# Three edits to an eight-core decoder step: the bias matmul's rows, a run of matmuls in an early wait, and who scales the last output

## The chip, the cores and the metric

The kernel runs on all 8 cores of one Trainium2 chip. All cores run the same program on their own data, without talking to each other: core i has prompt i of 2,048 tokens and 16 of the 128 running sequences with 8 new tokens each, 2,176 tokens in all. The metric is the device time in microseconds of the slowest core. Before the change it is 1296.83 us, the median of 3 runs from 1296.55 to 1297.41.

## The reference

One step of a two-layer trunk of width 1024. Every sub-layer works on a normalised and modulated input, and its result goes back through a gate:

```python
def modulate(x, g, shift, scale):
    return rms_norm(x, g) * (1 + scale) + shift
# per layer i; sh, sc, g come from silu(c) @ w_ada[i] + b_ada[i]
h = modulate(x, norm_g[i, 0], sh1, sc1)
y = pool_mixer(...)  if i == 0 else  sgu_mixer(...)
x = x + g1 * y
h = modulate(x, norm_g[i, 1], sh2, sc2)
x = x + g2 * (relu(h @ w1) ** 2) @ w2          # w1 1024x4096, w2 4096x1024
# at the end
return rms_norm(x, final_g)
```

Layer 0 mixes tokens by trailing-window means. Layer 1 mixes them by the spatial gating mixer, whose first step matters here:

```python
z = jax.nn.gelu(h @ w_in + b_in)               # w_in 1024x2048, b_in 2048
u, v = jnp.split(z, 2, axis=-1)
v = layer_norm(v, ln_g, ln_b)
mixed = w_eff @ v + b_sp                       # per chunk of 128 tokens, causal
y = (u * mixed) @ w_out
```

## The kernel before, in words

The activations x stay in SBUF for the whole kernel, as 8 blocks of 128 channels by 2,176 tokens in float32. h lies beside it in bf16. The tokens are cut into five groups (`GR`): 0 of 384, 1 and 2 of 512, 3 of 384, and 4 of 384, of which the last 128 are the running sequences. Weights come in pieces of 128x4096 through a ring of six buffers, loaded by GpSimd's DMA queue (POOL) in the fixed order of `PIECES`. A piece can be asked for when the piece that had its buffer is used up.

No engine's order is written by hand. Every operation is a node with a cost, a due time (`S.base`, or the running clock `S.clk` of matmul work) and optionally an earliest time. `schedule()` simulates all engines with these costs and picks, on each engine, the node with the lowest due time among those that could start first. The result is a fixed order for each engine, with semaphore waits for the data dependences. The planner's times are not on the chip; only the order is.

The start: groups 0 and 1 of x and the modulation pieces are loaded. `ada_piece` is 32 matmuls of 17 columns over one piece, followed by vector operations that write `modT`. Pieces (0,2) and (0,3) are the first two, then comes the small piece `wpool`, and then (0,4) is the third. ScalarE multiplies the pooling weights by the modulation (line 885), into a ring buffer (`wAvb`), and `pool_mm` (line 858) uses them. `h2_prompt` then forms the input of the channel MLP, whose first piece of w1 is used by line 1019.

The middle: the channel MLP of each layer runs in 8 blocks of 512 hidden units, over the five groups (`mlp`). `mm1` (line 1019) is 4 chains of 8 matmuls; ScalarE applies ReLU (line 1025) and the square (line 1027). `mm2` (line 1045) is 8 chains of 4 matmuls, and VectorE adds each into x (line 755). `weave` interleaves the `mm1` of one group with the `mm2` of the group before.

`v_tile` computes the v half of the gating mixer for 128 tokens at a time, in two halves of 512 channels: 8 matmuls of 128 rows (line 1201), then one matmul that adds the bias row to every token (line 1203). Its stationary operand is one row of ones and its moving operand one row of 512 bias values. There are 17 tiles, so 34 such matmuls. `binv` is loaded by one DMA of one row (line 1143).

`stats` squares x on ScalarE and sums over channels by a matmul with ones. In the `summed` form GpSimd adds the 8 squares in float32 (line 644), and a single matmul follows (line 646). In the other form 8 matmuls take the 8 squares (line 652). ScalarE's Ln and Exp give the reciprocal root: in PSUM for the summed form (lines 658 and 661), in SBUF for the other (`rstd` or `R1s`, lines 671 and 674).

The end: the last block goes over the groups in the order 4, 1, 2, 0, 3. After `mm2` of a group comes `final` for it: `stats`, then on VectorE `x * final_g * R` for each of the 8 channel blocks (line 1327), and a DMA for each pair of blocks (line 1331). Group 3 is split there into 256 and 128 tokens.

Of the kernel before, what the change touches and what calls it, by code (L numbers as in the profile page):

```python
# [380 lines left out]
def c_act(n):  # L381
    return 0.07 + n * 0.00085
# [10 lines left out]
def c_stt(n):  # L393
    return 0.13 + n * 0.00103
# [14 lines left out]
def build_program():  # L409
# [29 lines left out]
    def sb(name, shape, dt):  # L439
        return nc.alloc_sbuf_tensor(name, list(shape), dt)  # L440
# [25 lines left out]
    def AR(lo, hi):  # L466
        return ("ar", lo, hi)
# [17 lines left out]
    def P_(v):  # L485
        return ps[v.slot].ap()
# [35 lines left out]
    S.op("sp", lambda e: e.dma_start(out=vecs.ap(), in_=d_vecs.ap()), writes=VR, stream="s_vecs", cost=0.1, nbytes=196608)  # L522
    S.op("dve", lambda e: e.memset(ones.ap(), 1.0), writes=[("ones", 0, 1)])
    S.op("dve", lambda e: e.memset(mhalf.ap(), -0.5), writes=[("mhalf", 0, 1)], cost=0.1)
    S.op("dve", lambda e: e.memset(epsd.ap(), float(D * EPS)), writes=[("epsd", 0, 1)], cost=0.1)
# [101 lines left out]

    def stats(t0, n, own=False, summed=False):

# [25 lines left out]
        ch = S.chain(mms, v)  # L655
        if summed:
            RK = [(v.key, 0, 1)]
            ev = S.op("act", lambda e: e.activation(out=P_(v)[:, 0:n], in_=P_(v)[:, 0:n], func=AF.Ln, bias=epsd.ap()[:, 0:1], scale=1.0),
                      reads=[(v.key, 0, 1), ("epsd", 0, 1)], writes=RK, cost=c_act(n), vbs=[v], table="ln")
            S.evac(ch, ev)  # L660
            ev.glue = S.op("act", lambda e: e.activation(out=P_(v)[:, 0:n], in_=P_(v)[:, 0:n], func=AF.Exp, scale=-0.5),
                           reads=RK, writes=RK, cost=c_act(n), vbs=[v], table="ln")
            return Bank(v, 0, n), RK
        ri = rsi[0]
# [84 lines left out]
    def resid(l, vG, v, dco, t0, n, s0, s1):  # L749
# [8 lines left out]
        if s1 > s0:  # L758
# [311 lines left out]
    def mlp(l, after=None, hooks=None, first=None):  # L1070
# [5 lines left out]
        for (b, g) in steps:  # L1076
# [17 lines left out]
            else:  # L1094
                m1 = mm1(l, b, (hb(g), n, 0), ao, n)
                m2 = mm2(l, b, t0, n if g < 4 else 256, 256 if g == 4 else 0, 384 if g == 4 else 0, ao, n, 0)
                weave(m1, pend)
                if b == 7 and prevg is not None and after is not None:
# [35 lines left out]
    def sgu_setup():  # L1134
# [48 lines left out]
    def v_tile(g, tt):  # L1183
# [12 lines left out]
        for hf in range(2):  # L1196
# [5 lines left out]
                    [(pvb.key, 0, 1)] + HK(c0, c0 + 128, [dc]), 512) for dc in range(NDC)]  # L1202
            mms.append((lambda e, hf=hf, v=v: e.matmul(P_(v), ones.ap()[0:1, :], binv[0:1, hf * 512:(hf + 1) * 512], start=False, stop=True),  # L1203
                        [AR(BINV, BINV + 2048), ("ones", 0, 1)], 512))
            ch = S.chain(mms, v, vbs=[pvb])
# [89 lines left out]
    def sgu():  # L1295
# [19 lines left out]
        norm(1, 1, 4)  # L1315

    def final(g, off=0, nn=None, own=False):
        t0, n = GR[g]
        t0 += off
        if nn is not None:  # L1320
            n = nn
        R, RK = stats(t0, n, own, summed=nn is None and g != 0)
        for d in range(0, NDC, 2):
            S.base = S.clk + 30.0
            for dc in (d, d + 1):
                xs = xT.ap()[:, dc, t0:t0 + n]
                S.op("dve", lambda e, xs=xs, dc=dc: e.scalar_tensor_tensor(out=xs, in0=xs, scalar=vcol(VFG + dc), in1=R.ap(), op0=ALU.mult, op1=ALU.mult),  # L1327
                     reads=XK(t0, t0 + n, [dc]) + RK + VR, writes=XK(t0, t0 + n, [dc]), cost=c_stt(n), vbs=R.vbs)
            oo = 8 * t0 + d * n
            S.base = None  # L1330
            S.op("sp", lambda e, d=d, oo=oo: e.dma_start(out=o_y.ap()[:, oo:oo + 2 * n].rearrange("p (c t) -> p c t", t=n), in_=xT.ap()[:, d:d + 2, t0:t0 + n]),
                 reads=XK(t0, t0 + n, [d, d + 1]), stream="o_y", cost=0.1, nbytes=1024 * n)
# [89 lines left out]
```

How the kernel before makes its waits and increments, by code:

```python
                def body(eng, ops=seq[e], e=e):  # L356
                    for n in ops:
                        ins = None
                        for (emit, w) in n.swaits:
                            for d in w:
                                eng.wait_ge(d.sigval[0], d.sigval[1])
                            ins = emit(eng)
                        if n.stream is not None:
                            ins.then_inc(n.sigval[0], 16)
                        elif n.sig:
                            ins.then_inc(n.sigval[0], 1)
                    if e == "sp":
                        for (sem, val) in final:
                            eng.wait_ge(sem, val)
                        for e2 in ENGS:
                            if e2 != e and cnt[e2] > 0:
                                eng.wait_ge(esem[e2], cnt[e2])
```

## Time and profile before

| | before |
|---|---|
| median of 3 runs | 1296.83 us |
| the profiled execution's own time | 1297.52 us |
| its span, slowest core (5) | 1295.9 us |
| spans of the 8 cores | 1293.8 to 1295.9 us |
| busy: TensorE | 95% |
| busy: VectorE | 60% |
| busy: ScalarE | 45% |
| busy: GpSimd | 11% |

The span is the time from the first to the last instruction of a core; 1.6 us of the execution lie around it. The profile cuts the span into 40 slices of 32.4 us:

```profile
PE   2689999999999999999999999999999999999995
DVE  3488775544455454569777768754545455454577
ACT  3367543333333333377444666433333333333474
PEclk9799999999999999999999999999999999999997
DMA  9999586535253433311100035420303031200025
```

Each digit is a busy share in tenths; PEclk is the granted clock of TensorE. The first three slices and the last have an idle TensorE, and the DMA engines are busy throughout the first four. All rows below are of core 5, the slowest, unless they say otherwise.

### The profile page before, as it was taken

What the parts mean: (1) busy time and instruction counts of PE and PEld (TensorE: products, weight loads), DVE (VectorE), ACT (ScalarE), POOL (GpSimd) and SP (SyncE); (2) the same over time, 40 slices, a digit from 0 to 9 for tenths busy, and PEclk for the clock granted to TensorE, in tenths of its full rate; (3) what the DMA queues carried; (4) which work ended last, traced back from release to release, by engine and by line L of the source; (5) the groups of instructions that cost most, each with busy time, mean ns of one, the idle gap of its engine ahead of it and who ended that gap; (6) DMA issues with size and microseconds to landing.
All of it is one profiled execution on the core that took longest, in us unless ns stands there. A gap on an engine that the chain in (4) does not pass through costs nothing.

```text
span 1295.9 us, 21767 instructions; the slowest of 8 cores (1293.8 to 1295.9 us)
## 1 busy us (share of the span) xinstructions
PE 1236.4 (95%) x7481; PEld 662.2 (51%) x7481; DVE 771.3 (60%) x1482; ACT 584.1 (45%) x1084; POOL 138.5 (11%) x169
## 2 busy tenths in 40 slices
PE   2689999999999999999999999999999999999995
PEld 0345565555555555545444455554555555454543
DVE  3488775544455454569777768754545455454577
ACT  3367543333333333377444666433333333333474
POOL 2100000000000000055221230000000000000060
PEclk9799999999999999999999999999999999999997
DMA  9999586535253433311100035420303031200025
GB/s 199 215 215 171 90 121 102 95 61 89 51 95 58 73 66 66 66 33 34 33 1 1 1 65 97 100 47 19 66 1 66 1 65 31 35 2 1 1 88 190
DMA packets 20842, 91.08 MB, mean 70 GB/s; under 512 B 2768, under 2 KB 7168, under 8 KB 12656
## 3 DMA queue, kind: packets, MB, share of 16 engines
q0 software_dynamic: 11552, 76.26, 33.3%
q1 hardware_dynamic: 9184, 13.43, 3.5%
q8 instruction: 64, 1.05, 0.3%
q14 instruction: 42, 0.34, 0.1%
HBM read 145.43 MB, written 11.01 MB: 121 GB/s over the span
## 4 chain that ended last, share of the span: by engine, by line
PE 89%; DVE 3%; DMA 3%; issue 2%; ACT 1%; POOL 1%; DVEq 0%; ACTq 0%; POOLq 0%
PE ps L1019 36%; PE ps L1045 35%; PE ps L1288 5%; PE ps L1201 4%; PE ps L1171 3%; DMA ring<-w_pack 3%; PE ps L858 2%; PE ps L652 1%; PE ps L595 1%; PE ps L1203 1%; DVE hT_sb L721 1%; DVE xT_sb L1327 1%; DVE hT_sb L708 1%; PE ps L1254 1%; DVE xT_sb L755 1%
## 5 line engine op out<-in xcount | busy, mean ns | idle before, releaser
L755 DVE SCALAR_TENSOR_TENSOR xT_sb<-ps,modT,xT_sb 128x384 f32<-128x384 f32 (+3 forms) x728 | 458.2, 637 | 426.0 <-PE ps L1045 379.5
L1019 PE MATMUL ps<-hT_sb,ring 128*128 128x384 bf16 (+2 forms) x2592 | 522.1, 346 | 2.8 <-ACT hT_sb L718 2.5
L1045 PE MATMUL ps<-arena,ring 128*128 128x384 bf16 (+3 forms) x2624 | 522.3, 343 | 1.7 <-DVE xT_sb L755 1.6
L1025 ACT ACTIVATE arena<-ps 128x384 bf16<-128x384 f32 (+3 forms) x324 | 170.0, 527 | 490.8 <-PE ps L1019 490.8
L1045 PEld LDWEIGHTS ps<-arena,ring 128*128 128x128 bf16 x2624 | 253.7, 98 | 218.2 <-issue 3.2
L1019 PEld LDWEIGHTS ps<-hT_sb,ring 128*128 128x128 bf16 x2592 | 251.4, 98 | 220.6 <-issue 5.1
L1027 ACT ACTIVATE arena<-arena 128x384 bf16<-128x384 bf16 (+3 forms) x324 | 181.2, 562 | 27.2
L570 POOL DMA_DIRECT2D ring<-w_pack x62 | 33.3, 538 | 850.0 <-PE ps L595 336.3
L644 POOL TENSOR_TENSOR sq<-sq 128x512 f32<-128x512 f32 (+3 forms) x77 | 88.7, 1152 | 181.6 <-ACT sq L640 175.7
L640 ACT ACTIVATE sq<-xT_sb 128x512 f32<-128x512 f32 (+1 forms) x88 | 50.3, 579 | 47.0 <-DVE xT_sb L755 31.8
L649 ACT ACTIVATE sq<-xT_sb 128x384 bf16<-128x384 f32 (+3 forms) x128 | 57.9, 500 | 22.2 <-DVE xT_sb L755 15.2
L1201 PE MATMUL ps<-ring,hT_sb 128*128 128x512 bf16 x272 | 64.4, 380 | 0.0
L1171 PE MATMUL ps<-hT_sb,ring 128*128 128x384 bf16 (+1 forms) x320 | 62.6, 347 | 0.0
L1288 PE MATMUL ps<-arena,ring 128*128 128x384 bf16 (+1 forms) x320 | 60.0, 347 | 0.0
L708 DVE TENSOR_TENSOR hT_sb<-xT_sb,rstd 128x768 bf16<-128x768 f32 (+2 forms) x48 | 44.3, 973 | 17.6 <-ACT rstd L674 17.6
L652 PE MATMUL ps<-sq,ones 128*128 128x384 bf16 (+3 forms) x128 | 27.9, 339 | 22.1 <-ACT sq L649 20.6
L1288 PEld LDWEIGHTS ps<-arena,ring 128*128 128x128 bf16 x320 | 31.1, 98 | 27.8 <-issue 0.7
L768 DVE TENSOR_TENSOR xT_sb<-xT_sb,arena 128x128 f32<-128x128 f32 x136 | 40.2, 298 | 7.0 <-DVE arena L765 0.9
L1171 PEld LDWEIGHTS ps<-hT_sb,ring 128*128 128x128 bf16 x320 | 30.6, 98 | 25.3 <-issue 0.5
L718 ACT ACTIVATE hT_sb<-hT_sb,modT 128x384 bf16<-128x384 bf16 (+2 forms) x60 | 39.6, 723 | 5.2 <-DVE modT L603 2.7
L1201 PEld LDWEIGHTS ps<-ring,hT_sb 128*128 128x128 bf16 x272 | 24.6, 98 | 29.3 <-issue 4.3
L765 DVE TENSOR_TENSOR arena<-ps,modT 128x128 f32<-128x128 f32 x136 | 38.0, 281 | 2.7 <-PE ps L1045 2.6
(103 smaller groups left out, 533.0 us busy)
## 6 DMA issues: line engine op xcount, KB each, us to landing
ring<-w_pack POOLq DMA_DIRECT2D x62, 1024.0 KB, 10.3
xT_sb<-x_pack POOLq DMA_DIRECT2D x3, 1536.0 KB, 39.1
xT_sb<-x_pack POOLq DMA_DIRECT2D x2, 2048.0 KB, 35.1
y_pack<-xT_sb SPq DMA_DIRECT2D x8, 512.0 KB, 2.8
y_pack<-xT_sb SPq DMA_DIRECT2D x8, 384.0 KB, 3.0
ring<-w_pool POOLq DMA_DIRECT2D x1, 1024.0 KB, 33.3
y_pack<-xT_sb SPq DMA_DIRECT2D x4, 256.0 KB, 2.9
arena<-sp_pack POOLq DMA_DIRECT2D x1, 736.0 KB, 17.1
```

The lines of the kernel that those rows point to most:

```text
L640: S.op("act", lambda e, si=si, dc=dc: e.activation(out=fs[si], in_=xT.ap()[:, dc, t0:t0 + n], func=AF.Square), reads=XK(t0, t0 + n, [dc]), ...
L644: S.op("pool", lambda e, si=si, o=o: e.tensor_tensor(out=o, in0=fs[a], in1=fs[si], op=ALU.add), reads=fk[a] + fk[si], writes=k, cost=c_poo ...
L649: S.op("act", lambda e, si=si, dc=dc: e.activation(out=sqt.ap()[:, si * 512:si * 512 + n], in_=xT.ap()[:, dc, t0:t0 + n], func=AF.Square), ...
L708: S.op("dve", lambda e, d=d: e.tensor_tensor(out=hT.ap()[:, d:d + step, c0:c0 + n], in0=xT.ap()[:, d:d + step, t0:t0 + n], in1=rb(R, step) ...
L755: nodes.append(S.op("dve", lambda e: e.scalar_tensor_tensor(out=xs, in0=P_(v)[:, 0:n], scalar=mcol(l, vG, dco), in1=xs, op0=ALU.mult, op1= ...
L1019: mms = [(lambda e, dc=dc: e.matmul(P_(v)[:, 0:n], pv(key, 512)[:, dc, fc * 128:(fc + 1) * 128], hT.ap()[:, dc, c0:c0 + n], start=(dc == 0 ...
L1025: ev = S.op("act", lambda e: e.activation(out=av, in_=P_(v)[:, 0:n], func=AF.Relu), reads=[(v.key, 0, 1)], writes=ak, cost=c_act(n), vbs=[v])
L1027: S.op("act", lambda e: e.activation(out=av, in_=av, func=AF.Square), reads=ak, writes=ak, cost=c_act(n) + 0.03)
L1045: mms.append((lambda e, fc=fc, av=av: e.matmul(P_(v)[:, 0:w], pv(key, 1024)[:, fc, dco * 128:(dco + 1) * 128], av, start=(fc == 0), stop=( ...
L1171: mms = [(lambda e, dc=dc, key=key, fc=fc, v=v: e.matmul(P_(v)[:, 0:n], pv(key, 512)[:, dc, (fc % 4) * 128:(fc % 4 + 1) * 128], hT.ap()[:, ...
L1201: mms = [(lambda e, dc=dc, key=key, v=v: e.matmul(P_(v), hT.ap()[:, dc, c0:c0 + 128], pv(key, 512)[:, dc, :], start=(dc == 0), stop=False) ...
L1288: mms.append((lambda e, cc=cc, uv=uv, key=key, dco=dco, v=v: e.matmul(P_(v)[:, 0:n], pv(key, 512)[:, cc, (dco % 4) * 128:(dco % 4 + 1) * 1 ...
```

## The change

- **Bias.** A new tile `first` of 128x128 has ones in row 0 and zeros elsewhere. It is the stationary operand of the bias matmul, in place of one row of ones. The moving operand is `binv` with 128 rows, which one DMA fills by reading the bias row 128 times.
- **Matmuls in a wait.** `keep_busy(32)` adds one chain of 32 matmuls of ones by ones, 512 columns each, into a PSUM bank that nobody reads. Its due and earliest time in the plan is 31.0, ahead of the third modulation piece (32.0).
- **Last output.** All `final` calls now keep R in PSUM. For group 2 the sum of squares no longer goes through GpSimd. For blocks 6 and 7 of group 2 and 4 to 7 of group 0, ScalarE multiplies by `final_g` and GpSimd by a second copy of R in SBUF; VectorE keeps the rest. In the last step of the last block `mm2` of group 0 runs ahead of `mm1` of group 3 and is no longer woven with it.

```diff
+    S.op("dve", lambda e: e.memset(first.ap(), 0.0), writes=[("first", 0, 1)], cost=0.2)
+    S.op("dve", lambda e: e.memset(first.ap()[0:1, :], 1.0), reads=[("first", 0, 1)], writes=[("first", 0, 1)], cost=0.1)
...
-    def stats(t0, n, own=False, summed=False):
+    def stats(t0, n, own=False, summed=False, bank=None, both=False):
...
-        if summed:
+        if summed if bank is None else bank:
             RK = [(v.key, 0, 1)]
             ev = S.op("act", lambda e: e.activation(out=P_(v)[:, 0:n], in_=P_(v)[:, 0:n], func=AF.Ln, bias=epsd.ap()[:, 0:1], scale=1.0),
...
+            if both:
+                ri = rsi[0]
+                rsi[0] = 1 - ri
+                ro, rk = rstd[ri].ap()[:, 0:n], [(("rstd", ri), 0, 512)]
+                ev.glue = S.op("act", lambda e: e.activation(out=ro, in_=P_(v)[:, 0:n], func=AF.Exp, scale=-0.5),
+                               reads=RK, writes=rk, cost=c_act(n), vbs=[v], table="ln")
+                ev = ev.glue
...
+    def keep_busy(k):
+
+        v = S.vb("ps")
+        S.chain([(lambda e, v=v: e.matmul(P_(v), ones.ap(), bcast(ones.ap(), [0, 4], [1, 128]), start=True, stop=True),
+                  [("ones", 0, 1)], 512) for _ in range(k)], v)
...
+    S.base, S.earliest = 31.0, 31.0
+    keep_busy(32)
+    S.earliest = 0.0
     for a, b in ((4, 32.0), (5, 36.0), (8, 57.0), (9, 63.0), (6, 70.0), (7, 77.0)):
...
-                weave(m1, pend)
+                if l == 1 and b == 7 and g == 3:
+                    for f in pend + m1:
+                        f()
+                else:
+                    weave(m1, pend)
...
-        S.op("pool", lambda e: e.dma_start(out=binv[0:1, :], in_=d_binv.ap()), writes=[AR(BINV, BINV + 2048)], stream="s_binv", cost=0.53, nbytes=4096)
+        S.op("pool", lambda e: e.dma_start(out=binv, in_=bass.AP(d_binv, 0, [[0, 128], [1, 1024]])), writes=[AR(BINV, BINV + 2048)], stream="s_binv", cost=0.53, nbytes=4096)
...
-            mms.append((lambda e, hf=hf, v=v: e.matmul(P_(v), ones.ap()[0:1, :], binv[0:1, hf * 512:(hf + 1) * 512], start=False, stop=True),
-                        [AR(BINV, BINV + 2048), ("ones", 0, 1)], 512))
+            mms.append((lambda e, hf=hf, v=v: e.matmul(P_(v), first.ap(), binv[:, hf * 512:(hf + 1) * 512], start=False, stop=True),
+                        [AR(BINV, BINV + 2048), ("first", 0, 1)], 512))
...
+    SHARE = {2: (6, 7), 0: (4, 5, 6, 7)}
...
-        R, RK = stats(t0, n, own, summed=nn is None and g != 0)
+        share = SHARE.get(g, ()) if nn is None else ()
+        if share:
+            (R, RK), (Rp, RPK) = stats(t0, n, summed=False, bank=True, both=True)
+        else:
+            R, RK = stats(t0, n, own, summed=nn is None and g in (4, 1), bank=True)
...
+                if dc in share:
+                    S.base = S.clk + 20.0
+                    S.op("act", lambda e, xs=xs, dc=dc: e.activation(out=xs, in_=xs, func=AF.Identity, scale=vcol(VFG + dc)),
+                         reads=xk + VR, writes=xk, cost=c_act(n) + 0.05)
+                    S.op("pool", lambda e, xs=xs: e.tensor_tensor(out=xs, in0=xs, in1=Rp.ap(), op=ALU.mult), reads=xk + RPK, writes=xk, cost=c_pool(n))
+                    S.base = S.clk + 30.0
+                    continue
```

## Rows read from the trace of the kernel before

**Rows 1.** The page: busy time by engine, and the chain that ended last by engine.

```profile
PE 1236.4 (95%) x7481; PEld 662.2 (51%) x7481; DVE 771.3 (60%) x1482; ACT 584.1 (45%) x1084; POOL 138.5 (11%) x169
...
PE 89%; DVE 3%; DMA 3%; issue 2%; ACT 1%; POOL 1%; DVEq 0%; ACTq 0%; POOLq 0%
```

**Rows 2.** TensorE's timeline: start us, us, instruction, count, and idle before with its releaser.

```profile
609.84 1.89 PE L1201 MATMUL ps<-ring,hT_sb 128*128 128x512 bf16 x8
611.66 0.39 PE L1203 MATMUL ps<-arena,ones 1*128 1x512 bf16 x1
611.98 1.90 PE L1201 MATMUL ps<-ring,hT_sb 128*128 128x512 bf16 x8
```

**Rows 3.** Line 1203: count, duration ns min/median/max, first and last start.

```profile
L1203 PE MATMUL ps<-arena,ones x34: 384/385/385, 611.7 to 778.0; 1*128 1x512 bf16 x34
```

**Rows 4.** TensorE's timeline: a lone matmul of 128 rows, and what follows it.

```profile
1266.71 0.38 PE L646 MATMUL ps<-sq,ones 128*128 128x512 bf16 x1
1266.93 1.46 PE L1045 MATMUL ps<-arena,ring 128*128 128x384 bf16 x8
```

**Rows 5.** TensorE's waits from 190 to 1260 us; and its timeline at 625.

```profile
PE ps L652 <- DVE arena L1272: 1.4, 1, 1.4
...
625.31 0.32 PE L646 MATMUL ps<-sq,ones 128*128 128x384 bf16 x1 [0.76 <-POOL sq L644]
```

**Rows 6.** TensorE's timeline around the third modulation piece.

```profile
34.85 1.00 PE L595 MATMUL ps<-siluT,ring 128*128 128x17 bf16 x32 [5.12 <-DMA ring<-w_pack]
45.05 1.00 PE L595 MATMUL ps<-siluT,ring 128*128 128x17 bf16 x32 [9.20 <-DMA ring<-w_pack]
46.91 0.48 PE L858 MATMUL ps<-hT_sb,ring 128*128 128x384 bf16 x1 [0.86 <-ACT ring L885]
```

**Rows 7.** Windows: length, TensorE busy (count), granted clock, DMA share, GB/s.

```profile
45.00:50.00 5.00, 3.77 (x44) 0.50 0.98 234
50.00:51.00 1.00, 1.00 (x9) 0.90 0.89 315
91.00:94.50 3.50, 3.50 (x14) 0.52 1.03 343
```

**Rows 8.** ScalarE's timeline: the pooling weights.

```profile
46.26 6.50 ACT L885 ACTIVATE ring<-ring,Aw 128x256 bf16<-128x256 f32 x16 [17.93 <-PE ps L595]
```

**Rows 9.** First w1 piece: GpSimd's issue, its landing (us), TensorE's first use.

```profile
55.18 0.53 POOL L570 DMA_DIRECT2D ring<-w_pack  x1 [1.36 <-PE ps L595]
...
ring<-w_pack POOLq DMA_DIRECT2D x1, 1024.0 KB, 34.9
...
90.24 4.42 PE L1019 MATMUL ps<-hT_sb,ring 128*128 128x384 bf16 x16 [2.50 <-ACT hT_sb L718]
```

**Rows 10.** The same first use on core 6, in TensorE's timeline.

```profile
88.94 2.76 PE L1019 MATMUL ps<-hT_sb,ring 128*128 128x384 bf16 x16 [2.35 <-DMA ring<-w_pack]
```

**Rows 11.** VectorE's timeline at the end.

```profile
1267.85 1.27 DVE L755 SCALAR_TENSOR_TENSOR xT_sb<-ps,modT,xT_sb 128x384 f32<-128x384 f32 x2 [1.55 <-PE ps L1045]
1269.03 2.06 DVE L1327 SCALAR_TENSOR_TENSOR xT_sb<-xT_sb,vecs_sb,ps 128x512 f32<-128x512 f32 x3
...
1275.99 3.33 DVE L755 SCALAR_TENSOR_TENSOR xT_sb<-ps,modT,xT_sb 128x256 f32<-128x256 f32 x11
...
1280.55 7.48 DVE L1327 SCALAR_TENSOR_TENSOR xT_sb<-xT_sb,vecs_sb,rstd 128x384 f32<-128x384 f32 x16
1287.95 2.18 DVE L1327 SCALAR_TENSOR_TENSOR xT_sb<-xT_sb,vecs_sb,R1s 128x128 f32<-128x128 f32 x8
```

**Rows 12.** TensorE's timeline at the end.

```profile
1280.67 1.41 PE L652 MATMUL ps<-sq,ones 128*128 128x128 bf16 x7 [1.25 <-ACT sq L649]
```

**Rows 13.** Groups by shape from 1180 us: count, busy us, mean ns, idle before.

```profile
L644 POOL TENSOR_TENSOR sq<-sq 128x512 f32<-128x512 f32 x12 | 15.3, 1274 | 8.1 <-ACT sq L640 7.0 <-POOL sq L644 0.8 <-ACT arena L1027 0.2
...
L661 ACT ACTIVATE ps<-ps 128x512 f32<-128x512 f32 x2 | 1.2, 582 | 0.2
```

**Rows 14.** Window: length, busy us (count) of PE, PEld, DVE, ACT, POOL, clock, DMA.

```profile
1261.50:1283.00 21.50, 19.29 (x147) 12.77 (x144) 19.24 (x40) 15.75 (x41) 2.74 (x3) 0.99 0.41 153
```

More of the change, by code:

```diff
@@ L450, in build_program @@
     ones = sb("ones", [128, 128], BF16)
+    first = sb("first", [128, 128], BF16)
     siluT = sb("siluT", [128, NDC, NSEQ], BF16)
@@ L660, in stats @@
             S.evac(ch, ev)
+            if both:
[5 more added lines that the diff above has]
+                ev = ev.glue
             ev.glue = S.op("act", lambda e: e.activation(out=P_(v)[:, 0:n], in_=P_(v)[:, 0:n], func=AF.Exp, scale=-0.5),
                            reads=RK, writes=RK, cost=c_act(n), vbs=[v], table="ln")
+            if both:
+                return (Bank(v, 0, n), RK), (Fixed(ro), rk)
             return Bank(v, 0, n), RK
@@ L1326, in final @@
                 xs = xT.ap()[:, dc, t0:t0 + n]
+                xk = XK(t0, t0 + n, [dc])
+                if dc in share:
[5 more added lines that the diff above has]
+                    continue
                 S.op("dve", lambda e, xs=xs, dc=dc: e.scalar_tensor_tensor(out=xs, in0=xs, scalar=vcol(VFG + dc), in1=R.ap(), op0=ALU.mult, op1=ALU.mult),
-                     reads=XK(t0, t0 + n, [dc]) + RK + VR, writes=XK(t0, t0 + n, [dc]), cost=c_stt(n), vbs=R.vbs)
+                     reads=xk + RK + VR, writes=xk, cost=c_stt(n), vbs=R.vbs)
             oo = 8 * t0 + d * n
```

## The prediction

> **What bounds the kernel now.** I read the page first: its busy shares and the chain that ended last. TensorE is busy 95% of the span and is 89% of the chain [rows 1]. So an edit counts where it shortens TensorE's own stream, or the two stretches in which TensorE waits: the start, and the end. The timelines of TensorE for the three places of the diff, its waits from 190 to 1260 us, and then the landings of the first loads tell what ends last in each. Between 190 and 1260 us TensorE waits twice only, 1.4 and 0.76 us [rows 5]. The profiled execution took 1297.52 us, 0.7 above the median of the runs; the sum is made against 1297.52 and 0.7 is taken off.
>
> **Part 1, the bias matmul.** The reader should see pitches, not durations, since matmuls overlap. Eight matmuls of 512 columns take 1.89 us with the last one's 0.379 in it, so their pitch is (1.89 - 0.38) / 7 = 0.216 us. From the first of them at 609.84 to the one-row matmul at 611.66 there are 1.82 us, 0.09 more than 8 x 0.216 = 1.73; and from there to the next matmul at 611.98 there are 0.32, 0.10 more than 0.216 [rows 2]. One bias matmul costs 0.41 us where one of 128 rows would cost 0.216. The row of a lone 128-row matmul among others supports this: 1266.71 to 1266.93 is 0.22 [rows 4]. The gain is 0.195 us each, and there are 34 [rows 3], 6.6 us in all. The first three (611.7, 613.8, 624.2) lie ahead of a matmul at 625.31 that already waited 0.76 us for GpSimd's sums; that chain does not come sooner, so their 0.6 us goes into a longer wait [rows 5]. 31 x 0.195 = 6.0 us is my term. The other wait of the stretch hangs on VectorE work that follows TensorE's, and moves with it. Ends for the range: 6.6 if nothing is absorbed; 3.0 if the 128-row form removes only the delay ahead of it (34 x 0.09). The DMA of 128 rows is asked for during layer 0's MLP, where the DMA engines are mostly idle, and its first use is the matmul at 611.66. The two memsets stand in a stretch in which VectorE is idle.
>
> Here a page speaks against the edit. The Trainium skill ("TensorE: Matmul & The Clock Gate", section "Why this matters for your kernels") says that a single matmul of 32 rows takes the same time as one of 128. By it this term would be 0. The durations agree with it (385 against 379 ns); the pitches do not. The skill's "TensorEngine Tiling (Array Packing)", section "Key Properties", says that changing the tiling mode drains the engine, which would fit the pitches.
>
> **Part 2, the 32 matmuls.** The second modulation piece ends at 35.85 and the third starts at 45.05, after 9.20 us of waiting for its load [rows 6]. By the plan's costs the 32 matmuls (6.9 us from 31.0) fit between these two, so I place them there. At the pitch of 0.216 they take 6.9 us, and each microsecond at half clock (1.2 of 2.4 GHz) adds half a microsecond. The granted clock is 0.50 from 45 to 50 and rises at about 50.1, 5 us after TensorE had begun at 45.05; the later fall at 91 to 94.5 lasted 3.4 us with TensorE busy throughout [rows 7]. So 3.4 to 5 us at half clock: 8.6 to 9.4 us, against 9.2. The third piece starts at most 0.2 us later. Ends: 6.9 if the clock is full at once, 13.8 if it never rises, which would make the piece 4.6 us late.
>
> What it gives: piece three takes 0.8 in place of 1.0 us, and the first pooling matmuls (0.48 us each for 384 columns at half clock, against 0.326 at full) run at full clock. These wait for ScalarE's 16 scalings in turn, 0.41 us each [rows 6, 8], so only part shows: some 1.2 us by 54 us. But that is given back. The first w1 piece is issued at 55.18 and lands 34.9 us later, at 90.1; TensorE starts on it at 90.24, after 2.50 us idle [rows 9]. On core 6 the same start is put down to the load itself [rows 10]. The DMA share is 0.9 to 1.0 all the while [rows 7], and the loads stand in one queue, so an earlier issue doesn't land earlier. My term is 0. Ends: -1.2 if the start at 90.24 is after all held by ScalarE; +3.3 if the clock never rises (4.6 late, less the 1.3 that TensorE could catch up of its 2.5 idle).
>
> [...]
>
> **Part 3, the last output.** VectorE is busy without a gap from 1267.85 to 1290.13, while TensorE ends at 1282.1 [rows 11, 12]. So VectorE ends last. It loses two scalings of 512 columns (2.06 / 3 = 0.69 us each) and four of 384. The 16 of 384 and 256 columns took 7.48 us, some 0.53 and 0.40 each [rows 11]. So 2 x 0.69 + 4 x 0.53 = 3.5 us go. R in PSUM rather than SBUF I price at 0: both are read now.
>
> TensorE gains work: group 2's sum takes 8 matmuls rather than one, 7 x 0.216 = 1.5 us, in a stretch with little idle time [rows 14]. The pitch at 384 columns is (1.46 - 0.33) / 7 = 0.162 us [rows 4, 6]. `mm2` of group 0 starts at 1261.5 as before and takes 32 of them, 5.2 us, unwoven; then `mm1` of group 3 takes 5.2. With the sums (1.7 and 1.3) the `mm2` of group 3 is complete 1.5 us later than by the same count before. VectorE, now served early with group 0's residuals and with R of group 2 (GpSimd's seven adds of 1.27 us go [rows 13]), runs dry near 1272 and starts again at about 1275.5 with group 3. From there it has 16 residual adds, 5.0 us (3.33 us for 11, rounded for the shapes), four scalings of group 0, 2.1, eight of 256 columns, 3.2, and eight of 128, 2.2 [rows 11]: 12.5 us, ending at 1288.0 against 1290.13. The term is 2.1 us. ScalarE gains two Exp and six scalings, at most 8 x 0.58 = 4.6 us (the price at 512 columns; five of the eight have 384), on top of 15.75 busy in a window of 21.5 [rows 13, 14]: it stays just under full, and what it defers feeds GpSimd only. GpSimd's four products of 384 columns, about 1.0 us each by its 1.27 for 512, end near 1281, ahead of VectorE. The 5.8 us from VectorE's end to the span's end (last transfers) stay.
>
> Ends: -4.0, if VectorE keeps up and only the last sum (1282.1, and 1.0 later), its Ln and Exp (0.8 by the same price) and its eight scalings (2.2) bound it; +1.5, if the path goes through TensorE and ScalarE, which are later by the seven matmuls.
>
> **Sum.** 1297.52 - 6.0 - 0 - 2.1 = 1289.4; less 0.7 is 1288.7 us.
>
> **Rivals.**
> 1. The clock's gain carries over the load: 1.2 us more, 1287.5. For it: row 90.24 names ScalarE. Against it: the landing 0.14 us before. 11%.
> 2. The tail gives nothing: ScalarE, nearly full, delays the squares of group 3, and R comes late by TensorE's extra 1.5 us. 1288.7 + 2.1 + 1.5 = 1292.3. For it: 20.3 of 21.5 us. 18%.
> 3. The rows of the bias matmul don't matter (something else in the group's end costs 0.2 us): 1288.7 + 6.0 = 1294.7. Against it: no such delay at the other chains' ends. 5%.
> 4. Slower: the plan is another one. The 32 matmuls shift the planner's times, another piece is asked for behind a long wait in GpSimd's queue, and lands late. A landing takes 10.3 us (median over the 62 of the page); one piece that is missed in full gives 1288.7 + 10.3 = 1299.0. It decides from 8 us of stall on. Against it: in the plan the 32 matmuls fill idle time, and TensorE waits for no load after 90.24 now. That the matmuls are placed behind the third piece, and so don't do what they say, belongs here too: they would hold up the pooling matmuls by up to 8 us, though at full clock, with some of it absorbed by 90. 4%.
>
> **How the numbers follow.** The forecast has 62%. The range takes in rivals 1 and 2 and the ends of the terms (all three at their good ends would be 11.8 us off, about 1285): 1285.3 to 1292.8. A change of 0.2% is 2.6 us, about what can be told here: faster means under 1294.2. Forecast and rivals 1 and 2 are faster (91%), rival 3 is the same, rival 4 mostly slower; 0.90, 0.06, 0.04.
>
> **What would show it.** Bias: matmuls of 128*128 whose pitch is 0.216 on both sides, the mixer's stretch 6 us shorter, and the wait at 625 near 1.3 us. Part 2: 32 matmuls from 35.9, the clock full by about 41, and the first use of w1 still within 0.2 us of its landing. Part 3: VectorE without a gap from about 1269.5 to 1282 (all 6 us earlier), and ending 8 us sooner than before. I am wrong if the start at 90 moves by over 1 us, or VectorE's end isn't 7 to 9 us sooner.

## The result and the profile after

| | time, us |
|---|---|
| before, median of the runs beside it | 1296.83 |
| after, median of 6 runs (1286.29 to 1287.75) | 1286.91 |
| after / before | 0.9924, 95% interval 0.9912 to 0.9936 |
| after, the profiled execution | 1287.61, span 1286.1 |
| predicted | 1288.7 (1285.3 to 1292.8) |

The change takes 9.9 us off. Every time of a kernel here is the median of its undisturbed runs; runs that took longer with a lower granted clock on some cores (one of before, 1541 us) are left out.

The page of after: busy time by engine, and the chain that ended last by engine, as in [rows 1]. TensorE has shed only 2.3 us of busy time, and that is a net figure: the 32 matmuls add some 9.5 us to it. The delay around the bias matmuls, which went, had counted as busy, since the profile's matmuls overlap (in [rows 2] the one of 611.66 lasts until 612.05, and the next starts at 611.98).

```profile
PE 1234.1 (96%) x7424; PEld 668.8 (52%) x7520; DVE 768.0 (60%) x1478; ACT 587.2 (46%) x1092; POOL 136.1 (11%) x168
...
PE 90%; DVE 3%; issue 2%; DMA 2%; ACT 1%; POOL 1%; DVEq 0%; ACTq 0%; POOLq 0%
```

**Bias matmul.** TensorE's timeline of after (slowest core, 6), to be held against [rows 2]: the line of `first` is the bias matmul. It starts 0.22 us after a matmul of 512 columns has started and is followed 0.22 us later, where it was 0.32; from the first of the eight at 611.26 to the bias matmul at 612.98 there are 1.72 us, where there were 1.82.

```profile
611.04 0.38 PE L1228 MATMUL ps<-arena,first 128*128 128x512 bf16 x1
611.26 1.89 PE L1226 MATMUL ps<-ring,hT_sb 128*128 128x512 bf16 x8
612.98 0.38 PE L1228 MATMUL ps<-arena,first 128*128 128x512 bf16 x1
613.20 3.62 PE L1196 MATMUL ps<-hT_sb,ring 128*128 128x512 bf16 x16
...
624.78 0.32 PE L649 MATMUL ps<-sq,ones 128*128 128x384 bf16 x1 [1.27 <-POOL sq L647]
```

The last line is the wait of [rows 5]: 0.76 us has become 1.27. The other wait of that stretch is as long as before (TensorE's waits from 190 to 1250 us, total, times, longest):

```profile
PE ps L655 <- DVE arena L1297: 1.4, 1, 1.4
PE ps L649 <- POOL sq L647: 1.3, 1, 1.3
```

**The start.** TensorE's timeline of after, as in [rows 6, 10]. L787 is the 32 matmuls, L598 the modulation pieces, L876 the pooling matmuls, L1040 `mm1`.

```profile
35.56 9.67 PE L787 MATMUL ps<-ones 128*128 128x512 bf16 x32
45.06 0.96 PE L598 MATMUL ps<-siluT,ring 128*128 128x17 bf16 x32
46.88 0.32 PE L876 MATMUL ps<-hT_sb,ring 128*128 128x384 bf16 x1 [0.86 <-ACT ring L903]
...
87.19 0.96 PE L598 MATMUL ps<-siluT,ring 128*128 128x17 bf16 x32
88.87 0.81 PE L1040 MATMUL ps<-hT_sb,ring 128*128 128x384 bf16 x4 [0.72 <-DVE modT L606]
```

Windows of after around them (length, busy of PE, PEld, DVE, ACT, POOL with counts, granted clock, DMA share, GB/s): half clock up to 41 us while TensorE is busy, then the full one.

```profile
36.00:41.00 5.00, 5.00 (x14) 1.78 (x13) 2.43 (x7) 0.00 (x0) 0.53 (x1) 0.51 1.05 185
41.00:45.00 4.00, 4.00 (x20) 1.83 (x19) 0.00 (x0) 0.00 (x0) 0.00 (x0) 1.00 1.01 158
```

**The end.** TensorE's and VectorE's timelines of after, to be held against [rows 11, 12]. L1066 is `mm2`; 1254.55 is the start of `mm2` of group 0 (1261.5 before). L767 is the residual add, L1366 VectorE's final scaling. VectorE runs dry at 1265.93, restarts at 1267.87 and ends at 1280.56, with no gap between. L1040 of 384 columns is `mm1` of group 3: 8 matmuls of it lie ahead of 1254.55, and 24 behind.

```profile
1253.25 1.46 PE L1040 MATMUL ps<-hT_sb,ring 128*128 128x384 bf16 x8
1254.55 1.46 PE L1066 MATMUL ps<-arena,ring 128*128 128x384 bf16 x8
...
1261.48 4.06 PE L1040 MATMUL ps<-hT_sb,ring 128*128 128x384 bf16 x24
...
1266.68 0.49 PE L1066 MATMUL ps<-arena,ring 128*128 128x256 bf16 x3
1267.50 5.11 PE L1066 MATMUL ps<-arena,ring 128*128 128x256 bf16 x61 [0.33 <-ACT arena L1048]
...
1275.01 1.41 PE L655 MATMUL ps<-sq,ones 128*128 128x128 bf16 x7 [1.19 <-ACT sq L652]
```

```profile
1262.56 3.37 DVE L1366 SCALAR_TENSOR_TENSOR xT_sb<-xT_sb,vecs_sb,ps 128x512 f32<-128x512 f32 x5
1267.87 1.36 DVE L767 SCALAR_TENSOR_TENSOR xT_sb<-ps,modT,xT_sb 128x256 f32<-128x256 f32 x3 [1.94 <-PE ps L1066]
...
1273.70 6.86 DVE L1366 SCALAR_TENSOR_TENSOR xT_sb<-xT_sb,vecs_sb,ps 128x384 f32<-128x384 f32 x19
```

The window that answers to [rows 14] (same columns), and GpSimd's products. ScalarE is busy 19.04 of 22.0 us; GpSimd ends at 1272.4, 8 us ahead of VectorE.

```profile
1254.50:1276.50 22.00, 20.35 (x153) 13.41 (x151) 18.93 (x41) 19.04 (x47) 6.39 (x6) 1.00 0.55 205
```

```profile
1259.33 2.51 POOL L1363 TENSOR_TENSOR xT_sb<-xT_sb,rstd 128x512 f32<-128x512 f32 x2 [14.51 <-ACT rstd L668]
1268.52 3.88 POOL L1363 TENSOR_TENSOR xT_sb<-xT_sb,rstd 128x384 f32<-128x384 f32 x4 [6.68 <-ACT rstd L668]
```

### The profile page after: what moved, and what is told of

It reads as the page before. It is cut to its first block, busy times and chain, and to the rows that moved or that the text cites. A ratio compares the mean times of both kernels' runs of the same rounds, so it can differ in the third digit from the quotient of the medians.

```text
span 1286.1 us, 21748 instructions; the slowest of 8 cores (1282.2 to 1286.1 us)
## 1 busy us (share of the span) xinstructions
PE 1234.1 (96%) x7424; PEld 668.8 (52%) x7520; DVE 768.0 (60%) x1478; ACT 587.2 (46%) x1092; POOL 136.1 (11%) x168
## 4 chain that ended last, share of the span: by engine, by line
PE 90%; DVE 3%; issue 2%; DMA 2%; ACT 1%; POOL 1%; DVEq 0%; ACTq 0%; POOLq 0%
PE ps L1066 36%; PE ps L1040 35%; PE ps L1313 5%; PE ps L1226 4%; PE ps L1196 4%; DMA ring<-w_pack 2%; PE ps L876 2%; PE ps L598 1%; PE ps L655 1%; PE ps L787 1%; DVE xT_sb L767 1%; DVE hT_sb L720 1%; PE ps L1228 1%; ACT sq L652 1%; PE ps L1279 1%
## 5 line engine op out<-in xcount | busy, mean ns | idle before, releaser
L767 DVE SCALAR_TENSOR_TENSOR xT_sb<-ps,modT,xT_sb 128x384 f32<-128x384 f32 (+3 forms) x728 | 458.2, 637 | 426.9 <-PE ps L1066 381.5
L1066 PE MATMUL ps<-arena,ring 128*128 128x384 bf16 (+3 forms) x2605 | 518.3, 342 | 3.5 <-DVE xT_sb L767 2.1
L1040 PE MATMUL ps<-hT_sb,ring 128*128 128x384 bf16 (+2 forms) x2539 | 514.7, 344 | 4.3 <-DVE modT L606 0.7
L1066 PEld LDWEIGHTS ps<-arena,ring 128*128 128x128 bf16 x2624 | 253.7, 98 | 218.2 <-issue 3.4
L1040 PEld LDWEIGHTS ps<-hT_sb,ring 128*128 128x128 bf16 x2592 | 250.9, 98 | 218.8 <-issue 3.1
L647 POOL TENSOR_TENSOR sq<-sq 128x384 f32<-128x384 f32 (+3 forms) x70 | 79.9, 1141 | 177.0 <-ACT sq L643 172.1
L652 ACT ACTIVATE sq<-xT_sb 128x384 bf16<-128x384 f32 (+3 forms) x136 | 62.9, 507 | 24.8 <-DVE xT_sb L767 17.9
L643 ACT ACTIVATE sq<-xT_sb 128x384 f32<-128x384 f32 (+1 forms) x80 | 45.3, 574 | 44.7 <-DVE xT_sb L767 28.9
```

The source lines that it names most:

```text
L643: S.op("act", lambda e, si=si, dc=dc: e.activation(out=fs[si], in_=xT.ap()[:, dc, t0:t0 + n], func=AF.Square), reads=XK(t0, t0 + n, [dc]), ...
L647: S.op("pool", lambda e, si=si, o=o: e.tensor_tensor(out=o, in0=fs[a], in1=fs[si], op=ALU.add), reads=fk[a] + fk[si], writes=k, cost=c_poo ...
L652: S.op("act", lambda e, si=si, dc=dc: e.activation(out=sqt.ap()[:, si * 512:si * 512 + n], in_=xT.ap()[:, dc, t0:t0 + n], func=AF.Square), ...
L767: nodes.append(S.op("dve", lambda e: e.scalar_tensor_tensor(out=xs, in0=P_(v)[:, 0:n], scalar=mcol(l, vG, dco), in1=xs, op0=ALU.mult, op1= ...
L1040: mms = [(lambda e, dc=dc: e.matmul(P_(v)[:, 0:n], pv(key, 512)[:, dc, fc * 128:(fc + 1) * 128], hT.ap()[:, dc, c0:c0 + n], start=(dc == 0 ...
L1066: mms.append((lambda e, fc=fc, av=av: e.matmul(P_(v)[:, 0:w], pv(key, 1024)[:, fc, dco * 128:(dco + 1) * 128], av, start=(fc == 0), stop=( ...
```

## Where the time went, by stage

Total times of one kernel scatter by up to 1.5 us, as much as some of the parts are worth. Two stretches scatter far less: the v stretch, from the first to the last matmul of `v_tile`, and the tail, from that last matmul to the end of the core's span. In one trace the tail is the same on most cores to within some hundredths of a microsecond (before: 517.86 to 517.90 on six of them). So each part is read there. All values are us, read from the timelines; the first four columns are medians over the eight cores of one trace, the fifth is the median of the runs. The trace of the 32 matmuls alone has, until the v stretch, two cores with a lower granted clock (last section); over its other six cores the first v tile starts at 607.4.

| kernel | start of first v tile | v stretch | tail to VectorE's end | tail to span's end | time |
|---|---|---|---|---|---|
| before | 608.4 | 168.19 | 512.10 | 517.87 | 1296.83 |
| after | 607.8 | 161.87 | 509.38 | 514.90 | 1286.91 |
| after, run again | 608.0 | 161.86 | 509.38 | 514.89 | 1287.36 |
| bias alone | 608.0 | 161.86 | 512.04 | 517.80 | 1290.28 |
| bias of 32 rows alone | 607.8 | 168.19 | 512.10 | 517.86 | 1296.52 |
| 32 matmuls alone | 607.7 | 168.19 | 512.11 | 517.88 | 1295.98 |
| last output alone | 607.8 | 168.19 | 509.49 | 515.00 | 1293.72 |
| after without the 32 matmuls | 608.3 | 161.86 | 509.47 | 514.99 | 1287.84 |
| no shared blocks | 607.2 | 161.87 | 510.95 | 516.49 | 1288.73 |
| woven again | 607.0 | 161.87 | 509.43 | 515.97 | 1288.05 |
| one R, in SBUF | 607.2 | 161.86 | 511.15 | 516.66 | 1288.78 |
| sum on GpSimd | 608.1 | 161.87 | 509.94 | 516.50 | 1288.61 |
| six blocks of group 0 | 607.9 | 161.86 | 509.76 | 516.00 | 1288.38 |
| sum on GpSimd, squares in hT | 607.1 | 161.86 | 508.63 | 514.17 | 1286.25 |

From before to after: v stretch -6.3, tail -3.0 (VectorE's end -2.7, what follows it -0.3: 5.8 to 5.5), start -0.6. That last number is no clean reading: the five kernels without the 32 matmuls have 607.8 to 608.4 in that column (608.1 in the mean), the nine with them 607.0 to 608.1 (607.5). The ranges overlap, and the kernels ran on several chips; the means are 0.5 us apart.

## The experiments

They ran in three groups, each on one chip beside runs of before: 1296.6 in the first, 1296.7 in the second, 1297.0 in the third. The first group has the four kernels of parts alone, which differ from the kernel before by the edit shown. The others differ from the kernel after: the second group has those without shared blocks, with the order woven again, with one R and with the sum on GpSimd, the third has the rest. The second group has no run of after, so its tails are held against after's on another chip. Two traces of after, from two chips, agree in the tail within 0.01 us (514.90 and 514.89).

**Each part alone.** First the bias matmul.

```diff
+    first = sb("first", [128, 128], BF16)
...
-            mms.append((lambda e, hf=hf, v=v: e.matmul(P_(v), ones.ap()[0:1, :], binv[0:1, hf * 512:(hf + 1) * 512], start=False, stop=True),
+            mms.append((lambda e, hf=hf, v=v: e.matmul(P_(v), first.ap(), binv[:, hf * 512:(hf + 1) * 512], start=False, stop=True),
...
```

The memsets of `first` and the DMA of 128 rows are in it, as in the whole change.

> The bias matmul of 128 rows alone. Theory: the price of the one-row form is the 0.2 us around it (0.09 ahead, 0.10 behind), so the stretch of the v tiles gets 6.0 to 6.6 us shorter and the time falls by about 6.0 us; the pitch on both sides of the bias matmul is 0.216 us. Rival (the rows do not matter): no change, pitch 0.41 us as before.

Measured 1290.28, ratio 0.9951 (0.9938 to 0.9963): -6.3 us. The v stretch is 6.33 us shorter and nothing else moves. Its wait at 624 is 1.3 us.

The same with the first 32 rows of the same tiles:

```diff
-            mms.append((lambda e, hf=hf, v=v: e.matmul(P_(v), first.ap(), binv[:, hf * 512:(hf + 1) * 512], start=False, stop=True),
+            mms.append((lambda e, hf=hf, v=v: e.matmul(P_(v), first.ap()[0:32, :], binv[0:32, hf * 512:(hf + 1) * 512], start=False, stop=True),
```

> As e1_bias, but the bias matmul has 32 rows (partitions 0 to 31 of the same two operands) rather than 128. Theory A (a matmul of fewer rows than the array's is another tiling mode, and each change of mode costs): the delays of 0.09 and 0.10 us around it stay, and the time is that of the kernel before. Theory B (one row, read from a single partition, is what is slow): pitch 0.216 us and a time as e1_bias, some 6 us below the kernel before.

Measured 1296.52, ratio 0.9999 (0.9989 to 1.0009): no gain. TensorE's timeline of this kernel (core 3); the 0.32 us on both sides and the 1.83 us from 610.36 to 612.19 are those of [rows 2]:

```profile
610.04 0.38 PE L1206 MATMUL ps<-arena,first 32*128 32x512 bf16 x1
610.36 1.90 PE L1204 MATMUL ps<-ring,hT_sb 128*128 128x512 bf16 x8
612.19 0.38 PE L1206 MATMUL ps<-arena,first 32*128 32x512 bf16 x1
612.50 3.63 PE L1174 MATMUL ps<-hT_sb,ring 128*128 128x512 bf16 x16
```

So it is neither the single row, nor the DMA, nor the other stationary operand: a matmul of 32 rows, or of one, among ones of 128 costs 0.20 us on its way in and out. The Trainium skill ("TensorEngine Tiling (Array Packing)", section "Key Properties") says that a switch of the tiling mode drains the engine; by it 32 rows would cost what one row costs, and the trace agrees: 0.32 us on either side with both, 0.22 with 128. That the 0.20 us are such a drain is not shown; the runs show only when they are paid.

The 32 matmuls alone:

```diff
...
+    S.base, S.earliest = 31.0, 31.0
+    keep_busy(32)
+    S.earliest = 0.0
```

> The 32 matmuls in the third modulation wait alone. Theory (the first w1 load sets the start of the first channel MLP): TensorE starts on w1 within 0.2 us of its landing on the cores that wait for it, and the time moves by 0, at most 0.5 us. Rival (the full clock's gain carries over the load): the time falls by 1.2 us or more.

Measured 1295.98, ratio 0.9997 (0.9987 to 1.0007): -0.6 us, which can't be told from nothing. Neither stretch moves in the median; on cores 2 and 3 VectorE's end is 1.7 and 2.0 us later, with a granted clock of 0.81 to 0.82 from 1262 to 1280 us (last section).

The last output alone (its part of the diff as shown ahead):

```diff
+    SHARE = {2: (6, 7), 0: (4, 5, 6, 7)}
```

> The last output scaling alone, with the other order of the last step. Theory: VectorE's end moves by what it loses less what it waits: 2.1 us by the prediction, 3.3 us by the trace of the changed kernel (the parts then add up to the whole: 6.3 + 0.6 + 3.3 = 10.2). Rival (ScalarE sets the end): no gain, up to 1.5 us slower.

Measured 1293.72, ratio 0.9978 (0.9969 to 0.9987): -2.9 us, all of it in the tail (-2.87). The three parts alone give -6.3 - 0.6 - 2.9 = -9.8, the whole -9.9: they add up.

**The start again, from the other side.** On one chip, after as it is, and after without the 32 matmuls:

```diff
...
-    S.base, S.earliest = 31.0, 31.0
-    keep_busy(32)
-    S.earliest = 0.0
```

> The changed kernel again, beside the next three on the same chip. It is the measure for them: 1286.9 us by its first runs.

> The changed kernel without the 32 matmuls. Theory A (the first w1 load sets the start of the first channel MLP on nearly every core): the same time within 0.3 us. Theory B (the load holds the first matmuls only; the vectors for the modulated input, which come sooner with TensorE at full clock, hold the rest): 0.5 to 1.0 us above the changed kernel.

Measured 1287.36 (0.9924, 0.9912 to 0.9937) and 1287.84 (0.9928, 0.9916 to 0.994). The difference is 0.5 us, again smaller than the intervals. The traces tell why it is small. The same stretch of TensorE's timeline, first of after run again, then of after without the 32 matmuls (core 7 of both; the first line of the first has only 22 of the modulation piece's 32 matmuls, those that lie in the window, and ends at 86.55):

```profile
85.85 0.70 PE L598 MATMUL ps<-siluT,ring 128*128 128x17 bf16 x22
89.12 3.36 PE L1040 MATMUL ps<-hT_sb,ring 128*128 128x384 bf16 x10 [2.56 <-DMA ring<-w_pack]
```

```profile
86.47 0.96 PE L598 MATMUL ps<-siluT,ring 128*128 128x17 bf16 x32
88.78 2.98 PE L1031 MATMUL ps<-hT_sb,ring 128*128 128x384 bf16 x16 [1.35 <-DVE xT_sb L767]
```

With the 32 matmuls the work ahead ends 0.9 us sooner (86.55 against 87.43), and the wait is 1.2 us longer. The second trace names VectorE as the releaser, but there too the load landed last, at 88.67, 0.11 us ahead of the first use. On all sixteen cores of these two traces the first use stands 0.11 to 0.18 us behind the landing, by the issue and the time to landing. With the 32 matmuls that load is asked for 1.0 us sooner (53.5 against 54.5 in the median over the cores) and lands at the same time (87.8 in both): what is won ahead of the load goes into a longer time in the queue.

It isn't so on every core of every kernel, though. Over the five kernels without the 32 matmuls, 9 of 40 cores start on w1 0.5 to 1.5 us after it has landed, because TensorE's own work ahead ends only then: on core 0 of before the load lands at 87.66, TensorE is busy until 88.02, and starts at 88.24. Over the nine kernels with them it is 1 of 68, where the four cores of the die with the clock of 0.81 (last section) are not counted. So on some cores TensorE's own stream does end last, and there the earlier work can show.

**The parts of the tail.** Each of these takes one piece of the third part back. First, no block is shared:

```diff
-    SHARE = {2: (6, 7), 0: (4, 5, 6, 7)}
+    SHARE = {}
```

> The changed kernel with nothing handed to ScalarE and GpSimd (no shared blocks); the new order of the last step, the 8 matmuls for group 2's sum and R in PSUM stay. Theory (VectorE's work after group 0's residuals sets the end): group 2's two blocks go into VectorE's idle time of some 3 us, group 0's four cost 4 x 0.53, so the time is 2.1 us above the changed kernel, 1289.0. Rival (the new order is what gives the gain): no more than 0.5 us above it.

Measured 1288.73 (0.9938, 0.9926 to 0.995). The tail is 1.6 us longer than after's, all at VectorE's end; 2.1 were expected. So 1.6 of the 3.0 us go with the six blocks, and the other 1.4 stay with the order, the sum of group 2 on TensorE and R in PSUM.

The order is woven again:

```diff
-                if l == 1 and b == 7 and g == 3:
-                    for f in pend + m1:
-                        f()
-                else:
-                    weave(m1, pend)
+                weave(m1, pend)
```

> The changed kernel with the last step woven as before (mm2 of group 0 with mm1 of group 3); the shared blocks stay. Theory (handing over is the gain, the order only feeds it): 0 to 1.5 us above the changed kernel, 1287.6. Rival (the order gives most of it): 3 us above, 1289.9.

Measured 1288.05 (0.9934, 0.9921 to 0.9947). VectorE ends as in after (509.43 against 509.38), and still the tail is 1.1 us longer. The last twelve output DMAs show it: duration of the issue in ns (min/median/max) with first and last start, and issue to landing; of after first, then of this kernel.

```profile
L1370 SPq DMA_DIRECT2D y_pack<-xT_sb x12: 372/372/425, 1270.5 to 1281.1; - x12
...
DMA to landing us min/median/max: 2.3/2.5/2.6
```

```profile
L1366 SPq DMA_DIRECT2D y_pack<-xT_sb x12: 371/542/974, 1271.0 to 1281.2; - x12
...
DMA to landing us min/median/max: 2.4/3.4/3.8
```

The transfers stand a little closer together (355 GB/s from 1275 to 1280, against 330), an issue takes up to 0.97 us in place of 0.37, and a landing 3.4 in place of 2.5. What the order gives lies behind VectorE, in the output queue.

Both readers take R from one copy in SBUF:

```diff
-            (R, RK), (Rp, RPK) = stats(t0, n, summed=False, bank=True, both=True)
+            R, RK = stats(t0, n, summed=False, bank=False)
+            Rp, RPK = R, RK
```

> The changed kernel, but R of groups 2 and 0 has one copy, in SBUF, and VectorE and GpSimd both read it; ScalarE's second Exp goes (0.5 us each). Theory A (VectorE and GpSimd do not disturb each other, as their rows before showed with R in PSUM): the same time, at most 0.5 us less. Theory B (VectorE with both tensor operands in SBUF and GpSimd get in each other's way): VectorE's 384-column scalings take more than 0.61 us while GpSimd works, or GpSimd's products more than 1.0, and the time rises by 0.5 to 2 us.

Measured 1288.78 (0.9938, 0.9925 to 0.9951): VectorE's end 1.8 us later than after's. VectorE's timeline of this kernel, in the stretches in which GpSimd multiplies too:

```profile
1259.43 1.53 DVE L1367 SCALAR_TENSOR_TENSOR xT_sb<-xT_sb,vecs_sb,rstd 128x512 f32<-128x512 f32 x1
...
1269.02 1.45 DVE L1367 SCALAR_TENSOR_TENSOR xT_sb<-xT_sb,vecs_sb,rstd 128x384 f32<-128x384 f32 x1 [0.18 <-ACT rstd L686]
...
1274.95 0.60 DVE L1367 SCALAR_TENSOR_TENSOR xT_sb<-xT_sb,vecs_sb,rstd 128x384 f32<-128x384 f32 x1
```

And GpSimd's groups by shape (count, busy us, mean ns, idle before), of this kernel and then of after:

```profile
L1364 POOL TENSOR_TENSOR xT_sb<-xT_sb,rstd 128x512 f32<-128x512 f32 x2 | 3.0, 1498 | 14.6 <-ACT rstd L686 14.6
```

```profile
L1363 POOL TENSOR_TENSOR xT_sb<-xT_sb,rstd 128x512 f32<-128x512 f32 x2 | 2.5, 1276 | 14.5 <-ACT rstd L668 14.5
```

The same scaling takes 0.60 us beside an idle GpSimd and 1.45 beside a busy one, and GpSimd's product 1.50 in place of 1.28. They disturb each other when both read their two tensors from SBUF. In after, VectorE reads R from PSUM, and its scaling of 512 columns within GpSimd's two products (1259.33 to 1261.84) takes what the others take:

```profile
1260.33 0.74 DVE L1366 SCALAR_TENSOR_TENSOR xT_sb<-xT_sb,vecs_sb,ps 128x512 f32<-128x512 f32 x1
```

So R in PSUM is no detail: without it the whole gain of the six blocks is gone (tail 516.66, against 516.49 with no block shared).

The sum of group 2 goes through GpSimd, as before the change:

```diff
-            (R, RK), (Rp, RPK) = stats(t0, n, summed=False, bank=True, both=True)
+            (R, RK), (Rp, RPK) = stats(t0, n, summed=g == 2, bank=True, both=True)
```

> The changed kernel, but group 2's squares are again summed by GpSimd and take one matmul. Theory (the 7 extra matmuls stand on TensorE's path, and VectorE starts on group 3 when TensorE does): 7 x 0.216 = 1.5 us below the changed kernel, 1285.4. Rival (VectorE sets the end whatever TensorE does, and R of group 2 comes later): no change or up to 1 us slower.

Measured 1288.61 (0.9937, 0.9925 to 0.9949); the tail is 1.6 us longer, 0.6 at VectorE's end and 1.0 behind it, where an issue again takes up to 0.98 us. The gain of 1.5 us that was expected did not come, and the loss is larger than the rival's. ScalarE's timeline of this kernel: it stands idle 1.90 us in front of a square, in the stretch in which it is the scarce engine.

```profile
1258.52 1.35 ACT L652 ACTIVATE sq<-xT_sb 128x384 bf16<-128x384 f32 x3 [1.90 <-DVE xT_sb L767]
```

Two more blocks of group 0 are shared:

```diff
-    SHARE = {2: (6, 7), 0: (4, 5, 6, 7)}
+    SHARE = {2: (6, 7), 0: (2, 3, 4, 5, 6, 7)}
```

> The changed kernel with six blocks of group 0 handed over in place of four. Theory (VectorE's work sets the end): it ends 2 x 0.53 = 1.06 us sooner, 1285.9. Rival (ScalarE, 19 of 22 us busy there, is full): squares and ReLUs come later, and the time is the same or up to 1 us more.

Measured 1288.38 (0.9934, 0.9922 to 0.9946), the tail 1.1 us longer: the rival's case. VectorE has less to do, but now waits for ScalarE's Exp, and TensorE waits 0.62 us for `mm2`'s operand, where it was 0.33. That accounts for 0.4 us, at VectorE's end; the other 0.7 lie behind it, where an issue takes up to 0.69 us and a landing 2.9. Both timelines of this kernel:

```profile
1275.32 5.29 DVE L1366 SCALAR_TENSOR_TENSOR xT_sb<-xT_sb,vecs_sb,ps 128x256 f32<-128x256 f32 x16 [0.46 <-ACT ps L671]
```

```profile
1267.48 5.59 PE L1066 MATMUL ps<-arena,ring 128*128 128x256 bf16 x61 [0.62 <-ACT arena L1048]
```

**The sum on GpSimd, without the wait.** The sum of group 2 goes through GpSimd, and the squares of `final` that TensorE sums go to the part of `hT` that is no longer needed, in place of the few slots of `sq`:

```diff
...
+            if col is None:
+                si = sq_slot()
+                so, sk = sqt.ap()[:, si * 512:si * 512 + n], [("sq", si * 1024, si * 1024 + 2 * n)]
+            else:
+                so, sk = hT.ap()[:, dc, col:col + n], HK(col, col + n, [dc])
...
+            (R, RK), (Rp, RPK) = stats(t0, n, summed=g == 2, bank=True, both=True, col=hb(g) + off)
```

> As e9_sum2, but the squares of the last sums are written to the columns of hT of their own group, which nobody reads any more, rather than to the sq tile that GpSimd's sums still use. Theory (in e9_sum2 group 0's squares waited 1.9 us for those sums to free the tile, and ScalarE then fell behind): TensorE's 1.5 us now reach the end, 1285.4 to 1286.4. Rival (the output transfers are the bound, as their stretched issues in e9_sum2 say): no gain over the changed kernel.

Measured 1286.25 (0.9917, 0.9904 to 0.993), as expected, against 1287.36 of after on the same chip. By the times the two can't be told apart; by the tail this one is 0.7 us shorter (514.17 against 514.90), and 2.3 us shorter than with the sum on GpSimd and the squares in `sq`. ScalarE's and VectorE's timelines: ScalarE does six squares in a row where it had stood idle 1.90 us, and VectorE's last 19 scalings start at 1272.04 (1273.62 with the squares in `sq`, on a core whose first v tile is 0.3 us later). So what held that kernel back was the few slots of `sq`, which this edit takes away, and not the sum on GpSimd, which it keeps.

```profile
1256.27 2.98 ACT L656 ACTIVATE hT_sb<-xT_sb 128x384 bf16<-128x384 f32 x6
```

```profile
1265.90 1.79 DVE L771 SCALAR_TENSOR_TENSOR xT_sb<-ps,modT,xT_sb 128x256 f32<-128x256 f32 x4
...
1272.04 6.85 DVE L1370 SCALAR_TENSOR_TENSOR xT_sb<-xT_sb,vecs_sb,ps 128x384 f32<-128x384 f32 x19
```

## Why the prediction was right, point by point

The total was 1.8 us short of the measured change, of which the bias term has 0.3, the tail 0.9, and the start 0.6, if that is no scatter. All three miss to the same side, so the total isn't right by errors that cancel. The range held the time.

**Part 1.** Predicted 31 x 0.195 = 6.0; measured 6.3. The reading of pitches in place of durations was right: durations are 379 and 385 ns, and by them there would have been nothing to gain. The wait at 625 grew from 0.76 to 1.27, as forecast (1.3), so the first three gave nothing, and 34 x 0.20 - 0.5 is 6.3: the delay was 0.20 rather than 0.195 each. The lower end of the range (only the delay ahead of the matmul, 3.0) is out: the pitch is 0.22 on both sides. Rival 3 is out by the kernel with the bias part alone. The rule of the Trainium skill that the prediction names beside it ("TensorE: Matmul & The Clock Gate", section "Why this matters for your kernels": 32 rows take what 128 take) is borne out for one matmul's duration (385 against 379 ns), and not for what a matmul costs among others of 128 rows (0.41 against 0.22 us).

**Part 2.** Predicted 0; measured -0.6 and -0.5 in the two comparisons that take it alone, neither of them outside its interval. The matmuls came where I had put them, at 35.56 behind the second piece. They took 9.50 us to the third, 0.1 more than my longer estimate of 8.6 to 9.4; the clock was full by 41, as forecast. The third piece had landed at 44.6 (issued at 5.16, 39.4 us to landing) and started at 45.06, 0.5 us late where I had said 0.2 at most. Little of this shows, since on most cores the w1 load ends last, and an earlier issue doesn't land earlier, as the prediction had it. Rival 1 (the gain carries over the load, 1.2 us) is therefore not what happened in full. Its lower half stays inside the intervals, and something speaks for it: on 9 of the 40 cores without the 32 matmuls TensorE starts on w1 well after the landing, both comparisons go the same way, and the first v tile starts 0.5 us sooner in the mean of the kernels with them. The prediction shows the start on w1 for two cores and takes it for all. Whether the true value is 0 or 0.6 stays open.

**Part 3.** Predicted -2.1; measured -3.0. The path was the one forecast: VectorE dry, then held by group 3, then full to the end. From the start of `mm2` of group 0 it restarted after 13.3 us (predicted 14.0) and then had 12.7 us of work (12.5), so it ended 26.0 us after that start in place of 28.6. The step that was mis-sized is the one in which VectorE's restart is TensorE's stream counted up. I had all 32 matmuls of `mm1` of group 3 (5.2 us) behind the start of `mm2` of group 0; 8 of them still ran ahead of it, at 1253.25, so `mm2` of group 3 starts 12.1 us after that of group 0 (1254.55 to 1266.68) and not 13.4 (5.2 + 5.2 + 1.7 + 1.3). Half of that 1.3 is lost again, since VectorE restarts 1.2 us behind TensorE there, where I had 0.6. The seven added matmuls cost nearly what I said (1.5): TensorE's last sum starts 20.46 us after `mm2` of group 0, 1.3 later than before (19.2). The other term I had held fixed: the 5.8 us behind VectorE's end became 5.5. The experiments put sizes on what I had priced at 0 or left unpriced: the order is worth 1.1 us, nearly all in the output queue; the sum on TensorE 1.6, though it costs TensorE 1.3, since it spares ScalarE a wait of 1.9; R in PSUM 1.8. Each is what the kernel after loses without it; together with the 1.6 of the shared blocks they are twice the part's 3.0, so they hang on each other and don't add up. Priced at 0 was right for R in PSUM against what VectorE read before; against the other way of sharing it is the largest term.

Rival 2 (ScalarE full, the tail gives nothing) is out by the last output alone, -2.9 us. Its mechanism is one step away: with two blocks more VectorE waits for ScalarE's Exp, and the tail is 1.1 us longer. Rival 4 is out: TensorE waits for no load between 190 and 1250 us, as before.

Of the two signs of being wrong, both showed in part. VectorE's end was to be 7 to 9 us sooner: it is 9.6 on the slowest cores (1290.13 to 1280.56), 9.9 in the median over the cores, which is the tail's missing 0.9 once more. The start at 90 was not to move by over 1 us: between the slowest cores it moved from 90.24 to 88.87, but these are two different cores, and in the median over the cores it moved by 0.5 (88.2 to 87.7), as the landing did (87.9 to 87.5).

## What to carry to other kernels

Read pitches, from start to start, and not durations: a matmul of few rows between matmuls of 128 looks as cheap as any, and costs 0.20 us, which one of 128 rows with zeros in it doesn't. Before work is shared between VectorE and GpSimd, see that VectorE's second tensor lies in PSUM; and share only until the engine that feeds both is full. Time gained ahead of a load that ends last is lost at that load, whatever gained it; whether it ends last is to be read on every core, not on one.

## What the runs showed of the hardware

The disturbance between VectorE and GpSimd, 0.60 to 1.45 us for one scaling of 384 columns, was larger than I would have put at its upper end. Output transfers that crowd in the last 12 us lengthen the issuing instruction on SyncE as well, from 0.37 to 0.97 us. In the trace of the kernel with the 32 matmuls alone, two cores of one die, 0 and 1, had a granted clock of 0.81, between the two levels, from 60 to 150 us, while the other two of that die had 0.98 to 1.00; from 1262 to 1280 us it is these two that have 0.81 to 0.82, and cores 0 and 1 that have 1.00. Each core's times count from its own first instruction, so the trace doesn't tell whether the two stretches are one and the same of the die. The spans of cores 0 and 1 are 1311.7 and 1312.4 us, against 1291.6 to 1296.9 of the other six. Window of core 1 (columns as above):

```profile
60.00:70.00 10.00, 10.00 (x43) 4.47 (x42) 5.79 (x8) 6.73 (x13) 0.00 (x0) 0.81 1.03 173
```

The recorded clock can also miss half clock. In the trace of before, five of the eight cores (0, 2, 3, 6, 7) have a granted clock of 1.00 from 45 to 50 us, the others 0.50 to 0.52; on all eight a matmul of 384 columns there lasts 0.48 us, where it lasts 0.32 to 0.33 at full clock. So the durations decide.
